# A cap of two on the expert-weight transfers in flight, in a one-core MoE encoder kernel

## The chip, the cores and the metric

The kernel runs on one core of one Trainium2 chip. The metric is the device time of one execution in microseconds (us), lower is better. Three runs of the kernel before took 1706.2, 1709.3 and 1712.2 us, so the median is 1709.3 us. The profiled execution is the one of 1706.2 us; its span from the first to the last instruction is 1704.3 us.

## The reference

One layer of an encoder over 1024 tokens of 1024 features, in float32: adaLN conditioning, a token mixer (convolution, Fourier and gating heads) and a mixture of experts. The last part is what matters here:

```python
def expert_block(args):
    xb, e = args
    return (jax.nn.silu(xb @ w1[e]) * (xb @ w3[e])) @ w2[e]
...
y = jnp.zeros((N, D), h.dtype).at[t_s].add(contrib)      # two experts per token, weighted
...
x = x + gate2 * moe(h, ...)
return rmsnorm(x, final_g)
```

There are 64 experts. Each has w1 and w3 of 1024x512 and w2 of 512x1024, so 6 MB of float32 weights per expert and 384 MB in all. Each token picks one group of eight experts and the best two in it.

## The kernel before, in words

It is written by hand with one instruction stream per engine and semaphores between them. After the mixer and the router (up to about 510 us) comes the expert phase. The tokens of an expert are cut into **blocks** of 32 rows; every expert has at least one block, and there are 106 with these inputs. The expert phase has these streams:

- **SP** loads the weights. `piece(e, slot, k)` issues one DMA of 1024 KB into one of four slots of the arena: k = 0, 1 are the halves of w1, k = 2, 3 those of w3, k = 4, 5 those of w2. The first 24 pieces (four experts) are issued while the router still works. The loop at L374 issues the other 360, six for an expert: before k = 0 it waits until TensorE has used w1 and w3 of the expert that is in the slot (`s_h13`), before k = 4 until it has used w2 (`s_yp`). Each of the 24 places has its own semaphore, `s_w[slot][k]`. Nothing else limits how many pieces are under way. Behind the loop the same stream issues the 4 MB load of x2 (L387), the final gain, and the stores of the output.
- **GpSimd** gathers the rows of a block with an indirect DMA (L443), two blocks ahead.
- **TensorE** transposes the rows, multiplies them with w1 and w3 (`up`, L677, 64 matmuls), transposes the hidden rows (L694) and multiplies the hidden rows of the block before with w2 (`down`, L688, 32 matmuls). Before `down` it waits for `s_y`, which the next stream raises.
- **VectorE** at L1215 scales the result of a block out of PSUM into `y_s`. There is one `y_s`, so it waits first for `s_yst`, the landing of the store of the block before.
- **ScalarE** applies silu, copies, and at L846 issues the store of `y_s`, 128 KB, to `ys_dram`:

```python
act.dma_start(ys_dram.ap()[bass.ds(n * BLK, BLK), :].rearrange("r (q c) -> q r c", q=4), y_s).then_inc(s_yst, 16)
```

So a block has a loop through memory: L1215, store issued, store landed, L1215 of the next block. SP's pieces travel on DMA queue q1, ScalarE's stores on q10, GpSimd's gathers on q0. After the last block a tail gathers both results of each token, adds x2, normalises and writes the output.

Of the kernel before, what the change touches and what calls it, by code (L numbers as in the profile page):

```python
# [36 lines left out]
SLOTS = 4  # L37
# [2 lines left out]
EPS = 1e-6  # L40
BANKS = 8
EARLY = 4
NEG = -3.0e38

C_ID, C_TRI, C_ONE, C_BD, C_DFT, C_EXC, C_INC, C_REV = 0, 128, 256, 384, 512, 768, 832, 896
# [20 lines left out]
def build(nc, x, c, ln1_g, ln2_g, w_ada, b_ada, w_in, w_out, conv_w, conv_b, conv_gn_g, conv_gn_b,  # L66
# [3 lines left out]
    with ctx:  # L70
        def sem(name):
            return ctx.enter_context(nc.semaphore(name))
# [16 lines left out]
        def at(offset, *shape):  # L89
            n = 1  # L90
            for s in shape:
                n *= s
            view = arena[:, offset:offset + n]
            if len(shape) == 2:
                view = view.rearrange("p (a b) -> p a b", a=shape[0])
            if len(shape) == 3:
                view = view.rearrange("p (a b c) -> p a b c", a=shape[0], b=shape[1])
            return view
# [70 lines left out]
        prob, sel, sel2, hot1, hot2, cand, ranks, before = (at(r0 + i * HALF, HALF) for i in range(8))  # L169
# [43 lines left out]
        s_w = [[sem(f"slot{i}_{what}_in") for what in ("w1a", "w1b", "w3a", "w3b", "w2a", "w2b")] for i in range(SLOTS)]  # L213
# [74 lines left out]
        def _(sp):  # L288
# [25 lines left out]
            def piece(e, slot, k):  # L314
                u, h = k // 2, k % 2
                if u < 2:
                    src = (exp_w1, exp_w3)[u][bass.ds(e, 1), h * 512:(h + 1) * 512, :].rearrange("e (q p j) f -> (e p) q (j f)", q=2, j=2)
                else:
                    src = exp_w2[bass.ds(e, 1), h * 256:(h + 1) * 256, :].rearrange("e (k p) d -> (e p) k d", k=2)
                sp.dma_start(at(slot * EXPERT_FLOATS + k * 2048, 2, D), src).then_inc(s_w[slot][k], 16)  # L320
# [53 lines left out]
            with sp.Fori(0, EXPERTS // SLOTS - 1) as r:  # L374
                for slot in range(SLOTS):

                    end = sp.value_load(table[0:1, bass.ds(r * SLOTS + (1 + slot), 1)], min_val=1, max_val=MAX_BLOCKS)
                    for k in range(6):
                        if k == 0:
                            sp.wait_ge(s_h13, end)  # L380
                        if k == 4:
                            sp.wait_ge(s_yp, end)
                        piece(r * SLOTS + (SLOTS + slot), slot, k)

            end = sp.value_load(table[0:1, EXPERTS - SLOTS + 1:EXPERTS - SLOTS + 2], min_val=1, max_val=MAX_BLOCKS)
# [343 lines left out]
        def _(act):  # L729
# [80 lines left out]
            for i in range(TILES + 1):  # L810
# [5 lines left out]
                if i >= 1:  # L816
# [6 lines left out]
                    last.then_inc(freed_a, 1)  # L823
                if i == EARLY + 1:
                    act.wait_ge(s_expin, 1)
                    part = prob[:, 0:EARLY * EXPERTS]
                    nc.scalar.activation(part, part, ACT.Exp).then_inc(s_exp, 1)
            act.wait_ge(s_expin, 2)
            part = prob[:, EARLY * EXPERTS:]
            nc.scalar.activation(part, part, ACT.Exp).then_inc(s_exp, 1)  # L830
# [50 lines left out]
        def _(dve):  # L881
            steps = [0]

            def link(ins):

                steps[0] += 1
                ins.then_inc(s_link, 1)
                dve.wait_ge(s_link, steps[0])
# [146 lines left out]
            def route(part, t0, t1):  # L1035
# [3 lines left out]
                def tiles(view):  # L1039
                    return te(view)[:, t0:t1, :]  # L1040
# [27 lines left out]
                def first_best(values, top_row, hot, where_row):  # L1068

                    link(v.tensor_reduce(groups(top_row), tge(values), AX_X, ALU.max))  # L1070
                    link(v.tensor_tensor(tge(cand), tge(values), over_pe(top_row), ALU.is_equal))
                    link(v.tensor_tensor(tiles(cand), tiles(cand), over_t(cst[:, C_REV:C_REV + EXPERTS], n), ALU.mult))
                    link(v.tensor_reduce(groups(where_row), tge(cand), AX_X, ALU.max))
                    link(v.tensor_tensor(tge(hot), tge(cand), over_pe(where_row), ALU.is_equal))

                first_best(sel, 0, hot1, 1)
                link(v.scalar_tensor_tensor(tiles(sel2), tiles(hot1), NEG, tiles(sel), ALU.mult, ALU.add))
                first_best(sel2, 2, hot2, 3)
# [16 lines left out]
            def weights(t0, t1):  # L1095

                first, second, both = (tok[:, k, t0:t1] for k in (2, 3, 4))
                picked(first, prob, hot1, t0, t1)
                picked(second, prob, hot2, t0, t1)
                link(v.tensor_tensor(both, first, second, ALU.add))  # L1100
                link(v.reciprocal(both, both))
                v.tensor_tensor(gate_w[:, 0, t0:t1], first, both, ALU.mult)
                link(v.tensor_tensor(gate_w[:, 1, t0:t1], second, both, ALU.mult))
# [9 lines left out]
            for i in range(TILES + 2):  # L1113
# [25 lines left out]
                if i == 1:  # L1139
                    dve.wait_ge(s_gate2, 128)  # L1140
                    link(v.tensor_tensor(gate2, gate2, gate2_b, ALU.add))
                if i == EARLY + 1:
                    route(0, 0, EARLY)
                    weights(0, EARLY)

# [151 lines left out]
```

## Time and profile before

| what | value |
|---|---|
| median of three runs | 1709.3 us |
| profiled execution | 1706.2 us |
| its span | 1704.3 us |
| TensorE busy | 1242.9 us, 73% |
| VectorE, ScalarE, GpSimd busy | 27%, 12%, 11% |
| q1 (SP) over the span | 471.05 MB, 71.5% of 16 DMA engines |
| q0 (GpSimd) | 32.33 MB, 5.3% |
| q10 (ScalarE) | 13.90 MB, 2.4% |
| DMA share from 517 to 1620 us | 0.95 |
| granted TensorE clock, mean | 0.856 |

The expert phase reaches from about 510 to 1660 us and the tail from there to the end. The shares of the table are means over the whole span: in the expert phase the DMA engines are near full, before it they are half idle. TensorE is busy much of the time, but a busy TensorE is not one that sets the end; that is read from the chain and from the waits.

### The profile page before, as it was taken

The numbers are of one execution on the slowest core, as the hardware profiler recorded it, in microseconds if no ns is written. First come the engines' busy times: TensorE is split into PE (matmuls) and PEld (weight loads), VectorE is DVE, ScalarE is ACT, GpSimd is POOL, SyncE is SP. The second block draws the span as 40 slices with busy tenths as digits, with TensorE's granted clock in tenths as the row PEclk, the third lists the DMA queues.
The fourth block names the chain that finished last, engine by engine and source line by source line (L and its number), as shares of the span: only waits on it lengthen the run. The fifth ranks groups of instructions, "written<-read, shape, count | busy, mean of one in ns | idle before, by whom it ended". The sixth has DMA issues, their size and how long they took to land.

```text
span 1704.3 us, 31808 instructions
## 1 busy us (share of the span) xinstructions
PE 1242.9 (73%) x12648; PEld 658.3 (39%) x12649; DVE 456.3 (27%) x880; ACT 211.8 (12%) x537; POOL 186.2 (11%) x322
## 2 busy tenths in 40 slices
PE   3899999999837676667776787776666576776670
PEld 3444555445524333333433344333333233333330
DVE  1399936133641111111111111111111111111117
ACT  1400133012201000000100011000000000000014
POOL 3011300000001111011110111110110001110113
PEclk9999999999859888787977889777888778787985
DMA  9564523432489999897999958999999999799917
GB/s 334 196 208 162 216 85 135 152 118 99 165 336 358 392 357 411 337 398 281 363 410 385 376 216 348 366 410 410 376 374 375 377 387 372 291 408 411 394 64 295
DMA packets 156232, 517.73 MB, mean 304 GB/s; under 512 B 11865, under 2 KB 28777, under 8 KB 156072
## 3 DMA queue, kind: packets, MB, share of 16 engines
q1 hardware_dynamic: 130176, 471.05, 71.5%
q0 software_dynamic: 12032, 32.33, 5.3%
q10 hardware_dynamic: 13992, 13.90, 2.4%
q8 instruction: 24, 0.39, 0.1%
q14 instruction: 8, 0.07, 0.0%
HBM read 482.22 MB, written 35.01 MB: 303 GB/s over the span
## 4 chain that ended last, share of the span: by engine, by line
DMA 62%; PE 28%; DVE 5%; SPq 2%; issue 1%; ACT 1%; ACTq 0%; POOL 0%; POOLq 0%; DVEq 0%
DMA ys_dram<-arena 57%; PE banks L543 9%; PE banks L621 6%; PE banks L571 2%; DVE arena L1215 2%; SPq L320 2%; PE banks L589 2%; PE banks L688 1%; PE banks L677 1%; DMA arena<-in_exp_w 1%; DMA arena<-xh_dram,where 1%; DMA arena<-in_w_ada 1%; PE banks L491 1%; DMA arena<-in_x 1%; PE banks L637 1%
## 5 line engine op out<-in xcount | busy, mean ns | idle before, releaser
L677 PE MATMUL banks<-arena 128*32 128x256 f32 x6784 | 435.7, 414 | 92.3 <-DMA arena<-in_exp_w 55.3
L688 PE MATMUL banks<-arena 128*32 128x256 f32 x3392 | 292.3, 503 | 249.8 <-DVE arena L1215 249.7
L677 PEld LDWEIGHTS banks<-arena 128*32 128x32 f32 x6784 | 224.6, 119 | 273.4 <-issue 155.1
L688 PEld LDWEIGHTS banks<-arena 128*32 128x32 f32 x3392 | 141.0, 137 | 347.7 <-issue 318.4
L1215 DVE TENSOR_TENSOR arena<-banks,arena 128x256 f32<-128x256 f32 x106 | 45.1, 426 | 755.5 <-DMA ys_dram<-arena 746.1
L543 PE MATMUL banks<-arena 128*128 128x512 f32 x352 | 155.5, 600 | 6.9 <-ACT arena L778 6.9
L440 POOL COPY where<-quarters 128x1 int32 (+1 forms) x108 | 19.7, 182 | 1105.8 <-ACT arena L852 936.7
L838 ACT ACTIVATE arena<-banks 128x128 f32<-128x128 f32 x106 | 29.5, 278 | 797.3 <-issue 638.4
L965 DVE SCALAR_TENSOR_TENSOR arena<-arena 128x1024 f32<-128x1024 f32 x90 | 115.6, 1285 | 3.2
L443 POOL DMA_INDIRECT arena<-xh_dram,where x108 | 104.7, 969 | 87.7 <-POOL where L440 81.7
L621 PE MATMUL banks<-arena 128*128 128x512 f32 x256 | 111.4, 593 | 1.5 <-DVE arena L998 1.5
L543 PEld LDWEIGHTS banks<-arena 128*128 128x128 f32 x352 | 66.7, 192 | 89.0 <-issue 81.7
L1209 DVE TENSOR_TENSOR arena<-arena,banks 128x128 f32<-128x128 f32 x106 | 30.8, 290 | 230.7 <-ACT arena L838 230.7
L621 PEld LDWEIGHTS banks<-arena 128*128 128x128 f32 x256 | 48.1, 190 | 60.2 <-issue 57.6
L669 PE MATMUL banks<-arena 128*128 128x128 f32 x214 | 54.3, 336 | 9.1 <-ACT arena L852 9.1
L842 ACT ACTIVATE arena<-banks 128x128 f32<-128x128 f32 x106 | 29.5, 278 | 232.4 <-PE banks L694 232.4
L669 PEld LDWEIGHTS banks<-arena 128*128 128x128 f32 x214 | 33.6, 206 | 53.2 <-issue 53.2
L852 ACT ACTIVATE arena<-arena 128x256 f32<-128x256 f32 x108 | 44.8, 414 | 62.0 <-DMA arena<-xh_dram,where 61.8
L491 PE MATMUL banks<-arena 128*32 128x128 f32 x768 | 28.5, 311 | 28.1 <-DMA arena<-in_w_ada 25.6
L1202 DVE TENSOR_TENSOR arena<-banks,arena 128x256 f32<-128x256 f32 x107 | 44.8, 419 | 9.3 <-PE banks L669 9.2
L1205 DVE TENSOR_TENSOR arena<-arena 128x256 f32<-128x256 f32 x107 | 45.7, 427 | 3.7
L694 PEld LDWEIGHTS banks<-arena 128*128 128x128 f32 x106 | 16.7, 157 | 64.7 <-issue 55.2
(201 smaller groups left out, 692.9 us busy)
## 6 DMA issues: line engine op xcount, KB each, us to landing
arena<-in_exp_w SPq DMA_DIRECT2D x384, 1024.0 KB, 20.6
arena<-in_w_ada SPq DMA_DIRECT2D x12, 2048.0 KB, 11.6
ys_dram<-arena ACTq DMA_DIRECT2D x106, 128.0 KB
ys_dram<-arena POOLq DMA_DIRECT2D x16, 512.0 KB, 10.0
arena<-in_x SPq DMA_DIRECT2D x2, 2048.0 KB, 20.7
arena<-in_dft SPq DMA_DIRECT2D x1, 4096.0 KB, 12.6
arena<-in_w_out SPq DMA_DIRECT2D x1, 4096.0 KB, 14.0
arena<-in_x SPq DMA_DIRECT2D x8, 512.0 KB, 4.2
```

The source lines that it names most:

```text
L443: pool.indirect_dma_start(out=xrow_next, out_offset=None, in_=xh_dram.ap(), in_offset=bass.IndirectOffsetOnAxis(ap=where[:, 0:1], axis=0)) ...
L491: last = pe.matmul(ps[32 * q:32 * q + 32, 0:P], c_wide[:, k, :], ada_s[:, n % 2, k, q * P:(q + 1) * P], start=(k == 0), stop=(k == CH - 1) ...
L543: last = pe.matmul(ps, w_in_s[:, k, f0:f0 + P], h_t[:, k, s * HALF:(s + 1) * HALF], start=(k == 0), stop=(k == CH - 1))
L621: last = pe.matmul(ps, y_t[:, k, i * P:(i + 1) * P], w_out_s[:, k, s * HALF:(s + 1) * HALF], start=(n == 0), stop=(n == CH - 1))
L669: last = pe.transpose(xt_p[:, j * P:(j + 1) * P], xrow[:, j:QUART:2], ident)
L677: last = pe.matmul(h_p[32 * q:32 * q + 32, 0:2 * P].rearrange("p (a b) -> p a b", a=2), xt_s[:, k % 2, k // 2, :], w13[:, :, k, q * P:(q + ...
L688: last = pe.matmul(y_p[32 * q:32 * q + 32, 0:QUART], ff_t[:, k * BLK:(k + 1) * BLK], w2[:, k, q * QUART:(q + 1) * QUART], start=(k == 0), ...
L852: nc.scalar.activation(xrow, xrow_next, ACT.Copy).then_inc(s_xcopy, 1)
L965: ins = v.scalar_tensor_tensor(y_t[:, cc, :], src, w, y_t[:, cc, :], ALU.mult, ALU.add)
L1202: v.tensor_tensor(xt_v, banks[:, 0, 0:QUART].rearrange("p (a t) -> p a t", a=CH), ab_jq[:, 0, :, :].rearrange("p j q -> p (j q)").unsqueez ...
L1205: v.tensor_tensor(xt_v, xt_v, ab_jq[:, 1, :, :].rearrange("p j q -> p (j q)").unsqueeze(2).broadcast_to([P, CH, BLK]), ALU.add).then_inc(s ...
L1215: v.tensor_tensor(y_s, banks[:, 3, 0:QUART], gate2, ALU.mult).then_inc(s_y, 1)
```

## The change

Every piece that the loop issues first waits for the landing of the piece two places before it in the order of the stream. For k of 2 to 5 that is piece k - 2 of the same expert, for k of 0 and 1 it is piece 4 or 5 of the expert before (in the slot before, and for slot 0 in slot 3 of the round before, hence the other count). So at most two pieces of the loop are under way. The loads ahead of the loop and behind it are as they were.

```diff
+AHEAD = 2
...
                         if k == 4:
                             sp.wait_ge(s_yp, end)
+
+                        before, rounds = (slot, r + 2) if k >= AHEAD else ((slot - 1) % SLOTS, r + (2 if slot else 1))
+                        sp.wait_ge(s_w[before][(k - AHEAD) % 6], rounds * 16)
                         piece(r * SLOTS + (SLOTS + slot), slot, k)
```

On SP, the body of the loop for one expert (slot 0), before. The name block_h_ready is `s_h13`, block_y_filled is `s_yp`:

```order
L320 ISA [waits block_h_ready]
L320 DMA arena<-in_exp_w1 128x2x1024
L320 ISA
L320 DMA arena<-in_exp_w1 128x2x1024
L320 DMA arena<-in_exp_w3 128x2x1024 x2
L320 DMA arena<-in_exp_w2 128x2x1024 [waits block_y_filled]
L320 DMA arena<-in_exp_w2 128x2x1024
```

Two waits for six pieces. The same place on SP after the change; slot3_w2a_in and its like are `s_w[3][4]` and its like:

```order
L386 ISA [waits block_h_ready]
L321 ISA [waits slot3_w2a_in]
L321 DMA arena<-in_exp_w1 128x2x1024
L321 ISA [waits slot3_w2b_in]
L321 DMA arena<-in_exp_w1 128x2x1024
L386 ISA
L321 DMA arena<-in_exp_w3 128x2x1024 [waits slot0_w1a_in]
L321 DMA arena<-in_exp_w3 128x2x1024 [waits slot0_w1b_in]
L321 DMA arena<-in_exp_w2 128x2x1024 [waits slot0_w3a_in,block_y_filled]
L321 DMA arena<-in_exp_w2 128x2x1024 [waits slot0_w3b_in]
```

No DMA has moved and none was added; each of the six has a wait for a landing ahead of it. The lists of the other engines differ in line numbers alone.

## Rows read from the trace of the kernel before

**Rows 1.** The page's chain that ended last, shares of the span.
```profile
DMA ys_dram<-arena 57%; PE banks L543 9%; PE banks L621 6%; PE banks L571 2%; DVE arena L1215 2%; SPq L320 2%; PE banks L589 2%; PE banks L688 1%; PE banks L677 1%; DMA arena<-in_exp_w 1%; DMA arena<-xh_dram,where 1%; DMA arena<-in_w_ada 1%; PE banks L491 1%; DMA arena<-in_x 1%; PE banks L637 1%
```

**Rows 2.** Waits, 515 to 1640 us: total us, times, longest us.
```profile
DVE arena L1215 <- DMA ys_dram<-arena: 742.6, 96, 9.6
...
PE banks L677 <- DMA arena<-in_exp_w: 55.3, 9, 10.3
```

**Rows 3.** The chain in order of time: start us, length us, what.
```profile
562.99 11.09 DMA ys_dram<-arena
574.71 10.57 DMA ys_dram<-arena
...
804.74 8.80 DMA ys_dram<-arena
...
1653.59 3.32 DMA ys_dram<-arena
```

**Rows 4.** Issue to landing of the 384 weight pieces, us.
```profile
DMA to landing us min/median/max: 4.9/20.6/24.5
```

**Rows 5.** DMA queues, 802 to 803 us: packets, MB, share of 16 engines.
```profile
q10 hardware_dynamic: 86, 0.09, 25.2%
```

**Rows 6.** DMA queues, 563 to 566.8 us.
```profile
q1 hardware_dynamic: 403, 1.55, 102.1%
```

**Rows 7.** DMA queues, 566.8 to 573.5 us.
```profile
q1 hardware_dynamic: 647, 2.49, 92.2%
q10 hardware_dynamic: 130, 0.13, 5.5%
```

**Rows 8.** DMA queues, 804 to 805 us, then 804.7 to 808.8 us.
```profile
DMA packets 0, 0.00 MB, mean 0 GB/s; under 512 B 0, under 2 KB 0, under 8 KB 0
...
q1 hardware_dynamic: 305, 1.19, 90.3%
```

**Rows 9.** Issue to landing of the pieces issued at 452.5 and at 804.0 us.
```profile
DMA to landing us min/median/max: 4.9/4.9/4.9
...
DMA to landing us min/median/max: 5.3/5.3/5.3
```

**Rows 10.** The same for the piece issued at 455.2, and two at 456.1 and 456.7.
```profile
DMA to landing us min/median/max: 13.1/13.1/13.1
...
DMA to landing us min/median/max: 17.3/18.2/19.2
```

**Rows 11.** The same for the pieces issued at 1490.6 and 1595.9 (37 later).
```profile
DMA to landing us min/median/max: 16.6/16.6/16.6
...
DMA to landing us min/median/max: 21.5/21.5/21.5
```

**Rows 12.** The same for the pieces issued at 518.2 and 1599.1 (358 later).
```profile
DMA to landing us min/median/max: 8.8/8.8/8.8
...
DMA to landing us min/median/max: 20.8/20.8/20.8
```

**Rows 13.** Stores issued, 1500 to 1615 us, then 517 to 1614 us.
```profile
ys_dram<-arena ACTq DMA_DIRECT2D x10, 128.0 KB
...
ys_dram<-arena ACTq DMA_DIRECT2D x99, 128.0 KB
```

**Rows 14.** Issue to landing of the piece issued at 1593.6 us (k = 3 of the last expert).
```profile
DMA to landing us min/median/max: 20.4/20.4/20.4
```

**Rows 15.** TensorE in order of time, the last expert: start us, length us.
```profile
1621.90 3.66 PE L677 MATMUL banks<-arena 128*32 128x256 f32 x64
...
1633.85 4.37 PE L677 MATMUL banks<-arena 128*32 128x256 f32 x64
...
1640.71 3.66 PE L677 MATMUL banks<-arena 128*32 128x256 f32 x64
...
1646.86 3.66 PE L677 MATMUL banks<-arena 128*32 128x256 f32 x64
```

**Rows 16.** Issue of the x2 load, us to landing (issued at 1602.7 us).
```profile
arena<-x_dram SPq DMA_DIRECT2D x1, 4096.0 KB, 28.9
```

## The prediction

> **What bounds the kernel now.** I read the chain of waits first. Stores of block results hold 57% of it, and the weight pieces 1% [rows 1]. The waits say the same: in the expert phase VectorE's L1215 waits 742.6 us, 96 times, for the landing of the store before it, while TensorE waits only 55.3 us, 9 times, for weights [rows 2]. So the expert phase is a loop of store after store. A store that meets a full stream of weights takes 10.6 to 11.1 us from its issue to its landing, and the next starts 11.7 us after the one before; the store at 1653.59, with no weights under way, takes 3.3 us [rows 3]. The reader is to see that 128 KB cost 11 us because of what else is on the DMA engines.
>
> The second view is the queues. A weight piece lands 20.6 us after its issue in the median [rows 4], though pieces land 2.55 us apart (the piece of 455.2 lands at 468.3, that of 456.7, three later, at 475.9 [rows 10]). So some eight are under way, and the cap of two binds nearly always.
>
> What a store shares with them: alone on the queues it keeps 25.2% of 16 engines busy [rows 5], that is four engines, 86 packets in 1 us, 0.046 us each. Its 128 packets are thus 32 on each of four engines, 1.5 us of their time. A weight piece is 256 packets, 16 on each of 16 engines, 2.55 us, so 0.16 us each. In the first 3.8 us after the store of 562.99 no packet of q10 is served, and q1 has 403 [rows 6]; then q10 serves 130 within 6.7 us against 647 of q1 [rows 7]. On the four engines that is close to one for one: 32 pairs of 0.16 + 0.046 make 6.6 us. So a store first stands behind what those engines have already taken in (a store alone reaches them about 1.2 us after its issue, which leaves some 2.7 us, 17 packets of q1), then alternates with q1 for 31 more. By this, a store costs 3.3 + 48 x 0.16 = 11.0 us; the rows say 10.6 to 11.1.
>
> The four engines are also the bound of the weight stream. From the landing at 1507.2 to that at 1617.4 there are 37 pieces in 110.2 us [rows 11] and ten stores [rows 13]: 110.2 - 37 x 2.55 = 15.9, so 1.6 us for a store with its gather. The whole stream, 358 pieces from 526.9 to 1619.9 [rows 12], takes 1093 us; 358 x 2.55 = 913, and 99 stores [rows 13] x 1.6 = 158; the remaining 22 us are idle. For one expert (six pieces, 1.65 stores) the engines need 15.3 + 2.6 = 17.9 us, and the store loop 1.65 x 11.7 = 19.3 us. The two bounds lie close, the store loop slightly on top.
>
> **The change part by part.** Nothing but 360 waits on SP is new. Queued behind such a wait are the later pieces, and at the end the x2 load; no other engine's work stands on SP.
>
> *The store.* With two pieces under way, the four engines never hold more than 32 packets of q1. The landing is told about 0.5 us after the last data (4.9 us for a piece alone [rows 9], of which 1.0 us passes before the first packet, since there is none from 804 to 805 [rows 8], about 0.9 for the first, and 15 x 0.16). So at a landing 13 packets of the next piece are left; the new piece arrives 1.1 us later, when 6 are left. The backlog swings between 6 and 22, about 13 in the mean, where it was always above 17. While it is under 17 the store's packets fill the free places ahead of the next piece, about 10 of them; the other 22 alternate. So the store waits for 13 + 22 = 35 packets of q1 and not 48: 3.3 + 35 x 0.16 = 8.9 us, and the loop 9.5 us. Bounds: it could stay at 11.1, or come down to near 3.3. The nearest row is the store of 804.74, issued with just two pieces under way: 8.80 us [rows 3]. But those two were not followed by a third, and its first packet also came late, after 305 packets of q1 [rows 8], 19 on an engine.
>
> With a loop of 9.5 us, an expert needs 1.65 x 9.5 = 15.7 us of stores, under the 17.9 of the DMA engines. So the weights become the bound. The gain is not 96 x 2.2 us = 211 us but what the stream leaves idle: 22 us, of which I keep 5 for the stretches with many blocks for one expert. **-17 us.**
>
> *The handover.* A piece is issued when the one two ahead has landed, so two pieces take one latency and the wake of SP. A piece alone takes 4.9 to 5.3 us [rows 9]; SP I take at 0.1. That is 2.50 to 2.70 us for a piece against 2.55, a cost of 0 to 0.15, mean 0.08. While a store is on the four engines a piece takes 3.3 us and the new one comes in time, so nothing is lost. Stores cover some 60% of the time (6 of 10 us), which leaves 143 pieces: 143 x 0.08 = **+11 us**, bounds 0 and 21 (358 x 0.15 = 54 if the stores hide none of it).
>
> *The end.* The last expert's piece k = 3 lands at 1614.0 [rows 14], but its four up products start at 1621.9, 1633.9, 1640.7 and 1646.9 [rows 15]: the first 7.9 us late, behind the store loop, the second 12 us after it, the others at the 6.2 us that TensorE needs. With the faster loop the first starts as its piece lands; the second still meets the 4 MB x2 load, which lands at 1631.6 [rows 16], so I give it 10.5; then 7 and 6.2. The last starts 24 us after the landing and not 33: **-9 us**.
>
> Sum: -17 + 11 - 9 = -15. The profiled execution took 1706.2 us (span 1704.3), so 1691.2. It is 3 us under the median of the runs shown, 1709.3; I let the forecast stand between and say 1692.
>
> Here the rule that speaks against the change: the Trainium skill ("DMA: Bandwidth & Descriptors", Latency and other measured facts) says that the HBM access latency is 0.2 us in the mean and 2 us at high load, and that it makes up most of a DMA's fixed cost. No row here shows a piece that was issued alone into a loaded memory. By that rule the handover would be dearer than I take it, which is the first rival. The fit of the same page of the Trainium skill (Anatomy of one DMA, made for transfers that GpSimd issues), 2.0 us plus the bytes at 436 GB/s, would make it 4.4 us for a piece, an estimate, and the handover free.
>
> **The rivals.**
>
> *The queue runs dry (slower).* If the latency of a piece issued at a landing is longer under load than the 5.3 us of rows 9, each pair waits for it, in the stretches with stores too. With 6.3 us for a pair, 3.15 us for a piece, it is +0.6 x 143 = 86 us, less the 26 gained: 1766. The point from which it decides is 26 us: 0.18 us per piece outside stores, or 0.07 over all 358. For it: the margin is thin, 6 packets or 1 us of work when the new piece arrives, and the first packet of a piece takes 0.9 us. Against it: the range 4.9 to 5.3 includes exactly that. I take 1720 to 1770, centre 1735.
>
> *The store stays as it is.* If what a store waits for is only what the engines have taken in, and two pieces fill that (19 packets an engine were ahead of it with two under way [rows 8]), the loop stays near 11 us. Then the gains fall away and the handover stays: 1706 + 0 to 11, about 1711. Against it: the alternation needs a backlog behind the 17, and with two pieces there often is none.
>
> *The gain is larger.* If the handover is free and the stretches of idle go altogether: 1706.2 - 22 - 13 = 1671. Below that it can't go, since the engines' 913 + 158 us remain. Against it: three favourable ends at once.
>
> *The cap doesn't bind.* Excluded by the median of 20.6 us [rows 4]; no chance given.
>
> **How the numbers follow.** Forecast (1680 to 1702) 0.52; larger gain (1665 to 1680) 0.10; store unchanged (1703 to 1718) 0.17; queue runs dry (1715 to 1770) 0.21. What a measurement can tell from no change is 0.3%, 5 us: under 1704 is faster, over 1714 slower. Faster takes the first two and a sliver of the third: 0.63. Same: 0.14 from the third. Slower: 0.23. The range must leave out no more than 0.2: 1674 to 1728 leaves out part of the larger gain (0.04) and the upper part of the dry queue (0.14). The forecast's own range is 1680 to 1702.
>
> **What would show it.** Right: the pieces' median landing falls from 20.6 to 5 to 6 us; the stores in the chain take 8 to 9.5 us; L1215's wait for stores falls from 743 to below 500 us, and TensorE's wait for weights rises from 55 to over 150 us; pieces land 2.6 us apart outside stores, and the stream from 526.9 ends at about 1614. Wrong: stores still at 11 us (second rival), or stores shorter but pieces 2.8 us or more apart where no store is on, and the last landing later than 1620 (first rival). The DMA share of the expert phase would then fall, since the other twelve engines stand with the four.

## The result and the profile after

The changed kernel is slower. It takes 1834.5 us (1820.6 to 1842.3, 4 runs) against 1709.7 us (1706.2 to 1712.2, 4 runs), a ratio of 1.0727 [1.0673, 1.0781] (the brackets behind a ratio are its 95% interval). Thirteen more executions of the changed kernel took 1820.3 to 1854.8, so a capped kernel varies by some 1% from run to run, and the one before by 0.2%. I had said 1692, with a range up to 1728. Of the cases, the first rival had the direction ("the queue runs dry", 1720 to 1770), but its upper end too was short by 64 us.

The page of the changed kernel: the chain that ended last, which was 57% stores and 1% weights before [rows 1].

```profile
DMA arena<-in_exp_w 65%; PE banks L547 8%; PE banks L625 6%; PE banks L575 2%; PE banks L593 2%; DMA arena<-xh_dram,where 1%; PE banks L681 1%; PE banks L495 1%; DMA arena<-in_w_ada 1%; DMA ys_dram<-arena 1%; DMA arena<-in_x 1%; PE banks L641 1%; PE banks L692 1%; DVE arena L1249 0%; DVE arena L1244 0%
```

The weights have taken the chain from the stores. The waits of the changed kernel, 515 to 1790 us (total us, times, longest us), say the same. L681 and L1219 are the lines 677 and 1215 of before, moved by the four new lines:

```profile
PE banks L681 <- DMA arena<-in_exp_w: 430.1, 41, 15.5
DVE arena L1219 <- DMA ys_dram<-arena: 310.9, 63, 9.2
...
ACT arena L856 <- DMA arena<-xh_dram,where: 85.8, 41, 5.2
```

TensorE's wait for weights grew from 55.3 to 430.1 us, and VectorE's wait for stores fell from 742.6 to 310.9 [rows 2]. So the stores did get shorter, or at least less waited for, and it was no use. The weight pieces issued in the loop, and their time from issue to landing (20.6 us in the median before [rows 4]):

```profile
L321 SPq DMA_DIRECT2D arena<-in_exp_w x360: 15/373/386, 516.3 to 1755.5; - x180
...
DMA to landing us min/median/max: 4.8/7.0/9.3
```

The last issue is 359 pieces and 1239.2 us after the first: 3.45 us for a piece, where before it was 1093 / 358 = 3.05 [rows 12]. That is the whole loss. The last issue (k = 5 of the last expert) is released by the landing of the last expert's piece k = 3. It landed at 1614.0 before [rows 14], and now at 1755.5: +141.5 us. From there to the end of the span it was 1704.3 - 1614.0 = 90.3 us and is 1837.1 - 1755.5 = 81.6: -8.7. The sum, +132.8, is the difference of the two spans.

Where a piece loses its time is seen in the chain in order of time (start us, length us, what) of the changed kernel. Each row is a step from a landing to the landing of the piece that it released, so it moves two pieces:

```profile
612.17 7.36 DMA arena<-in_exp_w
...
619.55 5.36 DMA arena<-in_exp_w
...
625.07 5.20 DMA arena<-in_exp_w
...
630.28 8.73 DMA arena<-in_exp_w
...
639.03 5.04 DMA arena<-in_exp_w
...
644.23 4.92 DMA arena<-in_exp_w
...
649.17 7.17 DMA arena<-in_exp_w
...
656.36 7.52 DMA arena<-in_exp_w
```

Two kinds of step stand there. Four take 4.9 to 5.4 us, which is what 2 x 2.55 us of work need. The others take 7.2 to 8.7. The step of 8.73 us has a store in it (issued at 629.59) and a gather (630.83). I sorted all 358 such steps, from each issue to the next but one, by whether packets of a store or of a gather were served in them (worked out from the trace's packets): 218 have both, 7.3 us in the mean; 53 a store alone, 6.4; the other 87, nearly all with neither, 6.2. My sum had 6.6 for a step with a store and 5.26 without.

The DMA queues (packets, MB, share of 16 engines) of the changed kernel: at 623 to 626 us, ahead of that step and with no store on; inside it at 630.5 to 634.5, the store's first part; and at 635.1 to 635.9, just behind the issue of 634.94.

```profile
q1 hardware_dynamic: 313, 1.22, 102.9%
...
q1 hardware_dynamic: 363, 1.42, 94.5%
q10 hardware_dynamic: 100, 0.10, 7.4%
...
q1 hardware_dynamic: 18, 0.07, 22.4%
q10 hardware_dynamic: 8, 0.01, 2.9%
q0 software_dynamic: 4, 0.00, 1.5%
```

The reader is to see the last three rows: q1 falls to 22.4% of 16 engines, near the share of four. The trace has no engine numbers, so that they are the store's four is read from the share. The piece issued at 627.45 is told landed only just ahead of 634.94, 7.5 us later, since the issue of 634.94 waited for it. By then the packets show (worked out from the trace) that all but about four engines have run out of the next piece too, at about 634.5; the first packets of the newly issued one come at 636.0. So for 1.5 us twelve engines have nothing to do but a gather's packets, because the landing was held back by the four. Those first packets then take up to 0.89 us each, where a packet of q1 takes 0.16 in the median. Over the whole phase it shows in one row of the windows (after the length: busy us of PE, PEld, DVE, ACT and POOL, granted clock, DMA share, GB/s), first of the changed kernel and then of before:

```profile
517.00:1752.00 1235.00, 736.66 (x9999) 381.63 (x9999) 149.17 (x405) 92.50 (x304) 117.62 (x204) 0.78 0.92 325
```

```profile
517.00:1620.00 1103.00, 766.62 (x9997) 396.65 (x9993) 149.43 (x405) 89.33 (x304) 116.58 (x203) 0.83 0.95 369
```

The same matmuls and blocks, at 325 GB/s for 369. The share says more than that (worked out from the packets): of the 132 us that the window is longer, the engines stand for 52 and are busy for 80 with the same bytes. The 80 are long packets: about 4460 of q1 take over 0.3 us, 0.60 in the mean, where the kernel before has 1209. What they take over 0.16 us comes to 122 us for each engine, and to 33 before. The clock's fall from 0.83 to 0.78 is not the cause: TensorE is busy for 0.60 of the time and waits for data.

### The profile page after: what moved, and what is told of

Its sections match the earlier page's. It is cut to its first block, busy times and chain, and to the rows that moved or that the text cites. A ratio compares the mean times of both kernels' runs of the same rounds, so it can differ in the third digit from the quotient of the medians.

```text
span 1837.1 us, 31943 instructions
## 1 busy us (share of the span) xinstructions
PE 1213.9 (66%) x12648; PEld 643.2 (35%) x12649; DVE 456.3 (25%) x880; ACT 215.1 (12%) x537; POOL 186.7 (10%) x322
## 4 chain that ended last, share of the span: by engine, by line
DMA 69%; PE 25%; DVE 3%; issue 1%; ACT 1%; SPq 0%; POOL 0%; POOLq 0%; ACTq 0%; DVEq 0%
DMA arena<-in_exp_w 65%; PE banks L547 8%; PE banks L625 6%; PE banks L575 2%; PE banks L593 2%; DMA arena<-xh_dram,where 1%; PE banks L681 1%; PE banks L495 1%; DMA arena<-in_w_ada 1%; DMA ys_dram<-arena 1%; DMA arena<-in_x 1%; PE banks L641 1%; PE banks L692 1%; DVE arena L1249 0%; DVE arena L1244 0%
## 5 line engine op out<-in xcount | busy, mean ns | idle before, releaser
L681 PE MATMUL banks<-arena 128*32 128x256 f32 x6784 | 484.8, 448 | 462.3 <-DMA arena<-in_exp_w 430.1
L681 PEld LDWEIGHTS banks<-arena 128*32 128x32 f32 x6784 | 242.9, 128 | 671.8 <-issue 574.6
L692 PE MATMUL banks<-arena 128*32 128x256 f32 x3392 | 220.4, 403 | 37.2 <-DVE arena L1219 37.0
L692 PEld LDWEIGHTS banks<-arena 128*32 128x32 f32 x3392 | 108.9, 114 | 108.4 <-issue 50.2
L1219 DVE TENSOR_TENSOR arena<-banks,arena 128x256 f32<-128x256 f32 x106 | 45.1, 426 | 360.0 <-DMA ys_dram<-arena 310.9
L547 PEld LDWEIGHTS banks<-arena 128*128 128x128 f32 x352 | 66.7, 192 | 86.3 <-issue 81.9
L625 PEld LDWEIGHTS banks<-arena 128*128 128x128 f32 x256 | 48.1, 190 | 60.2 <-issue 57.9
L673 PEld LDWEIGHTS banks<-arena 128*128 128x128 f32 x214 | 33.6, 206 | 60.2 <-issue 49.6
L575 PE MATMUL banks<-arena 128*128 128x384 f32 x128 | 41.4, 486 | 0.0
## 6 DMA issues: line engine op xcount, KB each, us to landing
ys_dram<-arena POOLq DMA_DIRECT2D x16, 512.0 KB, 10.2
```

Source lines behind the costliest of these rows:

```text
L547: last = pe.matmul(ps, w_in_s[:, k, f0:f0 + P], h_t[:, k, s * HALF:(s + 1) * HALF], start=(k == 0), stop=(k == CH - 1))
L575: last = pe.matmul(ps[:, 0:SGU], h_t[:, k, i * P:(i + 1) * P], w_in_s[:, k, 1024 + SGU:WIN], start=(k == 0), stop=(k == CH - 1))
L625: last = pe.matmul(ps, y_t[:, k, i * P:(i + 1) * P], w_out_s[:, k, s * HALF:(s + 1) * HALF], start=(n == 0), stop=(n == CH - 1))
L673: last = pe.transpose(xt_p[:, j * P:(j + 1) * P], xrow[:, j:QUART:2], ident)
L681: last = pe.matmul(h_p[32 * q:32 * q + 32, 0:2 * P].rearrange("p (a b) -> p a b", a=2), xt_s[:, k % 2, k // 2, :], w13[:, :, k, q * P:(q + ...
L692: last = pe.matmul(y_p[32 * q:32 * q + 32, 0:QUART], ff_t[:, k * BLK:(k + 1) * BLK], w2[:, k, q * QUART:(q + 1) * QUART], start=(k == 0), ...
```

## The experiments

Two theories stood against each other. **A, unequal engines:** the store and the gather load some of the 16 DMA engines more than others; with two pieces under way those that are behind hold back the landing, the others run dry, and the 1 us of work that they have left is too little to cover it. **B, a fixed price:** the wait at each landing, or a latency that grows under load, costs some 0.4 us a piece, whatever else is on the engines.

**How many pieces.** AHEAD is the only edit; all waits stay.

```
-AHEAD = 2
+AHEAD = 3        (and, in the second kernel, 4)
```

> The cap of the change at 3 pieces instead of 2, nothing else. With the cap of 2 pairs of pieces take 7.3 us where a store and a gather run beside them (5.8 where none does), and the time is 1834 us. Theory A (unequal engines: a store lies on 4 of 16 engines and puts them behind, the landing waits for the last engine while the others run dry): a third piece gives every engine 2.55 us more of work, more than the 2 us by which engines drift, so most of the loss goes: pieces 3.0 us apart, about 1700 us. Theory B (a fixed latency of 7.1 us from issue to landing, divided by the number under way): 7.1/3 = 2.4 us, less than the 2.55 that the data take, so all of the loss goes and the shorter store stays: about 1690 us. If both are wrong and the loss is in SP's waits themselves, about 1830.

> The cap at 4. Theory A and theory B both: no loss of the stream is left; stores meet a backlog of more than 17 packets again and take 10.5 to 11 us, so 1700 to 1710 us, not told from the kernel before. If the waits themselves cost, over 1750.

Measured: 1710.9 us with three (ratio to before 0.9998 [0.9983, 1.0013]) and 1710.9 with four (0.9993 [0.9978, 1.0008]). The waits and landings with three, 515 to 1765 us:

```profile
DVE arena L1219 <- DMA ys_dram<-arena: 771.0, 98, 9.9
...
PE banks L681 <- DMA arena<-in_exp_w: 33.0, 6, 10.5
```

```profile
DMA to landing us min/median/max: 4.8/8.8/10.8
```

One piece more takes away the whole loss, and with it the form of B in which a wait costs something by itself: the same 360 waits cost nothing here. Both theories had the loss gone, so this run does not choose between them otherwise. It also takes away the gain, for which I had 1700 and 1690 on record. With 8.8 us to a landing the stores are waited for as long as before. None of the caps tried has both, a full stream and shorter stores.

**The store's shape.** The store's outer dimension has 4 elements. Here it has 128; the rows are then written in another order, which the result doesn't undo.

```
-act.dma_start(ys_dram.ap()[...].rearrange("r (q c) -> q r c", q=4), y_s)
+act.dma_start(ys_dram.ap()[...].rearrange("r (q c) -> (r q) c", q=4), y_s)
```

> The changed kernel (cap 2) with each block's result stored as one run of 128 rows of 1 KB, whose outer dimension is 128 instead of 4, so that it goes over 16 engines; the rows of the result land permuted, the bytes and their number are the same. Theory A: a store now takes 8 packets, 0.4 us, of every engine alike, so no engine is put behind: pairs with a store and a gather fall from 7.3 to about 6 us, the stream of 360 pieces from 1239 to about 1080 us, the time to about 1680 us. Theory B: the latency of a piece isn't due to where the store lies; pairs stay near 7 us and the time near 1800 us.

> The kernel before (no cap) with the same wide store. Both theories: the store takes 17 packets of q1 ahead plus 8 pairs, 1.2 + 2.7 + 8 x 0.2 + 0.7 = 6.2 us instead of 11, the loop 6.8 us; the stream needs 913 us + 99 x 0.7 (8 packets of the store and 2 of the gather per engine) = 982 us instead of 1093 with the idle of the long clusters. So about 1706 - 80 = 1625 us. If the four engines are not what bounds the stream, the time stays above 1680 us.

Measured: with the cap 1627.5 us (0.9521 [0.9458, 0.9583]), without it 1584.7 (0.9257 [0.9235, 0.9279]). The same bytes on 16 engines and not on four take 207 us from the capped kernel and 125 from the one before, where A had 1680 and 1625: the direction is A's, but both gains are 40 to 53 us larger than I had worked out. Waits, landings and chain of the capped one, the chain over the same part of the work:

```profile
PE banks L681 <- DMA arena<-in_exp_w: 298.3, 42, 11.3
...
DVE arena L1219 <- DMA ys_dram<-arena: 51.1, 28, 4.0
```

```profile
DMA to landing us min/median/max: 4.9/5.5/8.4
```

```profile
658.34 4.90 DMA arena<-in_exp_w
...
663.40 4.98 DMA arena<-in_exp_w
...
668.39 5.42 DMA arena<-in_exp_w
...
673.83 5.74 DMA arena<-in_exp_w
...
679.73 5.66 DMA arena<-in_exp_w
```

The steps of 7 to 9 us are rare now and the median landing falls from 7.0 to 5.5 us, with the same cap, the same waits and more bytes a second. So most of the loss is not a fixed price. It depends on where the store lies. But a cost of the cap stays that the store's shape doesn't explain, 1627.5 - 1584.7 = 43 us.

**Without the store, without the gather, without both.** The rows of the result are zeroed ahead of the phase, and a semaphore is raised in place of the store. For the gather, the blocks compute on stale rows.

```
-act.dma_start(ys_dram.ap()[...].rearrange("r (q c) -> q r c", q=4), y_s).then_inc(s_yst, 16)
+act.sem_inc(s_yst, 16)
-pool.indirect_dma_start(out=xrow_next, ..., in_=xh_dram.ap(), ...).then_inc(s_xrow, 16)
+pool.sem_inc(s_xrow, 16)
```

> The changed kernel (cap 2) without the stores of the block results in the expert phase (the semaphore is raised at once; the result rows are zeroed before the phase instead, 16 more 512 KB stores beside the mixer), so the result lacks the experts. Theory A (unequal engines): without the narrow store the pairs fall as they did with the wide one, from 7.3 to 5.9 us with a gather and to 5.0 without, and the time to about 1620 us. If the store only adds its own 1.5 us of work on four engines, which its wide form shares out, then 1836 us - 99 x 1.5 = 1685 us.

> The changed kernel (cap 2, narrow store) without the gathers of the blocks' rows (the semaphore is raised at once; every block computes on stale rows, the counts of blocks are the same). A gather is 2 packets, 0.32 us, of each engine. If it costs only that, 99 x 0.32 = 32 us less: 1805 us. If it costs what the pairs say (those with a store and a gather take 7.3 us, with a store alone 6.6, so 0.7 us for each pair that it touches, two pairs for most gathers), 0.7 us x 99: 1765 us. Theory A expects the latter or less, since the gather's packets too reach the engines at different times.

> The changed kernel (cap 2) with neither stores nor gathers in the expert phase. Only the weights are on the queues. Theory A: the handover itself is free, pairs take 5.05 us, as between stores with the wide store, and the stream of 360 pieces 905 us; the last block about 25 us later: 1706 - 190 = about 1510 us. The theory that each handover of two leaves a gap of its own (0.4 us per piece) gives 1050 us for the stream, 1650 us in all.

Measured, all with the cap of two: 1600.6 us without the store (0.9360 [0.9328, 0.9391]), 1767.2 and 1793.7 without the gather (two runs), 1561.1 and 1591.6 without both. So the store costs 1834 - 1601 = 234 us and the gather, beside it, 41 to 67; two runs so far apart don't tell its size better. For the kernel without the store I had 1620 by A and 1685 for a store that costs only its own 1.5 us. The waits without the gather:

```profile
PE banks L680 <- DMA arena<-in_exp_w: 376.4, 41, 16.0
...
DVE arena L1218 <- DMA ys_dram<-arena: 272.1, 61, 8.9
```

I had 1510 us on record for the kernel without both; it took 51 to 82 us more. The queues of it (the run of 1591.6), 515 to 1515 us, in 40 slices and in sum:

```profile
GB/s 299 378 406 406 406 395 399 346 304 343 308 342 386 364 385 405 404 407 408 404 398 390 322 371 407 409 349 325 349 318 383 405 357 371 369 408 403 393 399 409
DMA packets 97448, 375.78 MB, mean 376 GB/s; under 512 B 5728, under 2 KB 5728, under 8 KB 97442
```

Nothing but weights is on the engines here, and still the stream holds its 405 to 409 GB/s only in some stretches and has 300 to 350 in others. A step of two pieces takes 5.25 us in the median but 5.57 in the mean (2.78 for a piece), and 41 of 358 take 6.5 us or more (18 take 7). So two pieces are not enough even without any other load. That the engines can be kept full through the phase shows in a kernel further below, with three pieces under way and with stores and gathers spread over 16 engines. In 39 of 40 slices from 520 to 1490 us it stays at 401 GB/s or more (`cap3_four_stores`):

```profile
GB/s 401 410 409 409 409 410 409 409 409 408 409 409 410 409 409 409 409 409 380 410 409 409 409 408 409 408 409 409 409 408 409 409 409 408 409 409 409 409 410 409
```

A has no cause for the dips with two, unless the engines get out of step by themselves; B has one, if a latency comes and goes that a third piece hides. These runs don't tell the two apart.

**How much on the four engines.** The store still goes over four engines, but only the first 256 bytes of each 1024-byte row are written (the rest stays zero).

```
-...rearrange("r (q c) -> q r c", q=4), y_s)
+...rearrange("r (q c) -> q r c", q=4)[:, :, 0:QUART // 4], y_s[:, 0:QUART // 4])
```

> The changed kernel (cap 2) with the narrow store over the same four engines, but only the first quarter of each 1 KB row stored: 32 packets of 256 bytes an engine (the result rows are zeroed before the phase, so the result lacks the rest). Theory A: the four engines fall behind by some 0.5 us a store instead of 1.5, less than the margin of 1 us, so most of the loss goes: 1610 to 1650 us, near the wide store's 1628. If the number of packets or the fact of a store over four engines is what costs, and not how long it holds them, it stays above 1750 us.

Measured: 1643.3 us (0.9602 [0.9546, 0.9658]), two runs.

```profile
PE banks L681 <- DMA arena<-in_exp_w: 324.6, 42, 14.8
...
DVE arena L1219 <- DMA ys_dram<-arena: 68.6, 32, 6.9
```

By load on the four engines: none 1601, a quarter of the bytes 1643, all 1834 (1.5 us a store). The first quarter costs 43 us, the rest 191. A packet of 256 bytes takes 18 ns on its engine and one of 1024 takes 46 (medians of q10, worked out from the trace), so the small store holds its four engines for 32 x 0.018 = 0.6 us and the whole one for 1.5. The price is thus not in proportion: 0.6 us cost 43, and 0.9 us more cost 191. That is the steep rise that A expects where the hold grows past the 1 us of work that the other engines have left; one point in between doesn't show where it begins. It is not the number of packets, which is the same.

**Pieces of twice the size.** Two pieces of 2 MB under way hold the work of four of 1 MB.

```
-for k in range(6): ... piece(..., slot, k)
+for u in range(3): ... double(..., slot, u)      # 2 MB, one semaphore
```

> The changed kernel with the loop's pieces doubled to 2 MB (a whole w1, w3 or w2 of an expert in one DMA) and the cap still at two pieces. The store is the narrow one. Theory A (what matters is the work that each engine still has when a landing is told, against the drift between engines): 5.1 us of work remain, as with a cap of three of the small pieces, so no loss: about 1711 us. The rival, that two transfers under way are too few whatever their size because of the wait and the issue of each: half as many handovers at the same price each, 1709 + 125 / 2 = 1772 us.

Measured: 1748.4 us (1.0228 [1.0198, 1.0258]), slower than before by 2.3% and faster than the change. A had 1711 and the rival 1772. Its waits:

```profile
DVE arena L1226 <- DMA ys_dram<-arena: 811.3, 100, 10.4
PE banks L688 <- DMA arena<-in_exp_w: 27.2, 4, 10.8
```

TensorE waits 27.2 us for weights, so the stream is not what bounds it any more, as A says. But the store loop is longer than with three pieces of 1 MB: 811 us of waits and not 771, which is the 38 us between the two kernels. From its issue to its last packet a store takes 9.9 us in the mean here and 9.5 there (worked out from the packets), and there are about 100 of them. What makes it longer beside 2 MB pieces I did not find out.

**The complete kernel with a spread store.** Four DMAs of 32 rows of 1 KB put the same data at the same place over 16 engines, and their semaphore goes up by 64.

```
-act.dma_start(ys_dram.ap()[bass.ds(n * BLK, BLK), :].rearrange("r (q c) -> q r c", q=4), y_s).then_inc(s_yst, 16)
+for q in range(4):
+    act.dma_start(ys_dram.ap()[bass.ds(n * BLK, BLK), q * QUART:(q + 1) * QUART], y_s[32 * q:32 * q + 32, :]).then_inc(s_yst, 16)
```

> The kernel before (no cap), its result stored correctly by four DMAs of 32 rows each, one for each quarter of the columns, each over 16 engines (2 packets an engine), all landed before the buffer is written again. Theory A: the same 8 packets on every engine as the wide store, which took 1585 us, but ScalarE now issues four DMAs of 0.55 us, 1.65 us more in the loop of a block: stream near 982 us as before it, loop about 8.5 us, so 1590 to 1610 us. If four small DMAs cost more on the engines than one (each has its own semaphore packets and restarts), up to 1650 us.

> The cap at 3 and each result stored by four DMAs of 32 rows over all 16 engines (the version that took 1585 us without a cap); a complete kernel. Theory A: with no engine put behind and 5.1 us of work left at a landing the stream loses nothing; it took 991 us uncapped. Waits for gathers (167 us) and stores (184 us) may shrink with the backlog, but PE's wait for weights is the bound, so 1575 to 1590 us. If a cap has a cost of its own at any depth: 1600 to 1625 us.

> The cap at 2 and each result stored by four DMAs of 32 rows over all 16 engines: a complete kernel, the fourth corner beside the kernel before (1709), the change (1834) and four stores without a cap (1585). Theory A: the price of the cap falls from 125 us to what gathers and chance leave, as with the wide store, 43 us: about 1628 us, within 15. If each of the four store DMAs disturbs the 16 engines at another time, more: up to 1660 us. If the cap costs the same wherever the store lies: 1710 us.

Measured: 1585.0 us without a cap (0.9271 [0.9249, 0.9293]), 1585.6 with a cap of three (0.9268 [0.9242, 0.9293]), 1653.7 with two (0.9640 [0.9600, 0.9681]). All compute the whole reference, and the first, for which I had 1590 to 1610, beats both kernels of this case, the one before by 7.3%. Its waits and a window of it (columns as above; the kernel before has 0.95 and 366 GB/s in the same window, the changed one 0.91 and 323):

```profile
PE banks L677 <- DMA arena<-in_exp_w: 245.5, 37, 10.8
...
DVE arena L1216 <- DMA ys_dram<-arena: 183.6, 70, 4.4
ACT arena L853 <- DMA arena<-xh_dram,where: 167.3, 69, 4.1
```

```profile
520.00:1490.00 970.00, 689.29 (x9899) 361.63 (x9899) 147.23 (x399) 93.23 (x298) 115.31 (x199) 0.85 1.03 408
```

The wait for stores falls from 742.6 us [rows 2] to 183.6, and the stream runs at 408 GB/s, which is 1 MiB in 2.57 us: nothing is left for a cap to give. ScalarE pays for the four issues, one row of its timeline:

```profile
700.21 1.75 ACTq L847 DMA_DIRECT2D ys_dram<-arena  x4
```

The one issue took 0.56 us. The 1.2 us more are less than what each store saves. With two pieces, waits again:

```profile
PE banks L681 <- DMA arena<-in_exp_w: 324.3, 41, 15.1
...
DVE arena L1220 <- DMA ys_dram<-arena: 96.8, 54, 4.0
```

The price of a cap of two is thus 125 us with the narrow store, 69 with four spread ones and 43 with one; that of a cap of three is nothing with either. I had 1628 for the kernel behind the second of these, and up to 1660 in case four DMAs disturb the engines more than one with the same bytes. They do, by 26 us at a cap of two and by nothing without a cap (1585.0 and 1584.7), and I can't say why.

## Why the prediction was wrong

**What bounds the kernel: right.** Stores bound the loop, the four engines the stream close behind it. The experiment with a spread store shows both at once: the loop and the stream shrink together, and 125 us go. With the cap of three, where the stream is whole again, stores bound the loop as before. I had counted the 158 us that the stores and gathers take from the stream and left them alone, as a given.

**The store gets shorter: right in direction, and more than I had.** I had 11.0 us down to 8.9, by 2.1. From its issue to its last packet on the queue a store took 10.2 us before and takes 7.4 now (medians, worked out from the trace's packets), 2.8 less. The wait ahead of L1219 fell from 7.7 us in the mean to 310.9 / 63 = 4.9. For the loop I had 9.5 us; where it still waits it varies, as these rows of VectorE in the changed kernel show, 8.4 and 11.7 us apart (start, length, in brackets the wait):

```profile
1017.78 0.43 DVE L1219 TENSOR_TENSOR arena<-banks,arena 128x256 f32<-128x256 f32 x1 [5.36 <-DMA ys_dram<-arena]
1026.21 0.43 DVE L1219 TENSOR_TENSOR arena<-banks,arena 128x256 f32<-128x256 f32 x1 [5.52 <-DMA ys_dram<-arena]
1037.88 0.43 DVE L1219 TENSOR_TENSOR arena<-banks,arena 128x256 f32<-128x256 f32 x1 [8.77 <-DMA ys_dram<-arena]
```

**What the stream leaves idle, -17: it did not come.** It needed a stream that is full. The stream was no longer full, so the term went with the next one.

**The handover, +11: mis-sized, and the step that failed.** It reads: "While a store is on the four engines a piece takes 3.3 us and the new one comes in time, so nothing is lost." With it went "143 x 0.08" for the pieces outside the stores. Together with the -17 they gave a stream of 3.03 us a piece, 6.06 a step: 60% of the steps at 6.6 and 40% at 5.26. The steps measured are 76% with a store, at 7.14 in the mean, and 24% without, at 6.2 (6.91 over all). Per step that is

- 0.76 x (7.14 - 6.6) = 0.41 us because a step with a store is longer than the four engines' work,
- 0.24 x (6.2 - 5.26) = 0.23 because steps without one are longer too,
- 0.16 x (6.6 - 5.26) = 0.21 because more steps have a store in them than I had counted,

0.85 us in sum, and over 179.5 steps 73 + 41 + 38 = 152 us on top of my stream, which had the +11 and the -17 in it. My forecast of the profiled span was 1704.3 - 15 = 1689.3 us, and it is 1837.1, 148 more: these three terms account for it within a few us.

The first is the quoted step. The new piece comes in time for the four engines, which have a store's work on top of the piece's. It does not for the other twelve: the landing waits for the four, which need up to 1.5 us more, and 1.5 us is more than the 1 us of work left. So the twelve stand, which the rows at 635.1 show. The experiments show the cause from two sides: the loss goes with a third piece, and most of it goes when the store is spread or left out.

That twelve engines stand would alone leave the step at the pace of the four, 6.6 us; that these lose time as well is shown by the 7.14. What they lose it to is in part seen: the 80 us of longer packets are more than the 52 us of standing. A piece that finds empty engines has long first packets (0.70 to 1.1 us for the one issued at 804.0 in the kernel before, up to 0.89 for the one at 634.94 above), and the more often engines run dry, the more of these there are. I had this 0.9 us in the time of a lone piece, and nothing for engines that run dry inside the stream. That all the long packets are such restarts fits, but isn't shown.

For the second term, the kernel with neither store nor gather has 5.57: a lone piece's 4.9 to 5.3 us [rows 9], on which 0.08 rested, is too short for a step inside a stream, by 0.3 us of the 0.9.

**The end, -9: right in sum, by luck in its parts.** The four blocks of the last expert now start their up products 0.4 us after the landing at 1755.4 and then as here, TensorE in the changed kernel:

```profile
1755.82 5.26 PE L681 MATMUL banks<-arena 128*32 128x256 f32 x64 [9.90 <-DMA arena<-in_exp_w]
...
1763.58 3.66 PE L681 MATMUL banks<-arena 128*32 128x256 f32 x64
...
1769.73 3.66 PE L681 MATMUL banks<-arena 128*32 128x256 f32 x64
...
1779.38 3.74 PE L681 MATMUL banks<-arena 128*32 128x256 f32 x64
```

The last starts 23.9 us after the landing; I had 24. The steps in between are 7.8, 6.2 and 9.7 us, where I had 10.5, 7 and 6.2, so the errors cancel: the long store (11.0 us, issued at 1764.15) holds back the fourth block and not the second.

**The first rival** had the right outcome and a quarter of the mechanism, a latency that grows under load and costs most where no store is on. Its mark, 2.8 us or more a piece where no store is on, did come (3.1), but that is a quarter of the loss; most of it lies where the store is. The mark that named the cause is the last one: the DMA share falls, because twelve engines stand with the four. I wrote that sentence without asking what it does to the sum.

Two of my signs of being right came as well (VectorE's wait for stores below 500 us, at 310.9, and TensorE's for weights over 150, at 430.1): they were no use, since the slower outcome has them too.

Of the rule of the Trainium skill ("DMA: Bandwidth & Descriptors", Latency and other measured facts), 2 us of memory latency at high load, the weights alone show no constant sign: their median step of 5.25 us, in stretches at 406 GB/s, is no longer than with a lone piece's latency. The stretches at 300 to 350 GB/s it might explain; no run here tells.

**The second rival** (store unchanged, about 1711) is what a cap of three and of four do. In the rival with the larger gain the sum has 13 us for the end, where the part on the end has 9, and gives no row for it; nothing hangs on it.

## What to carry to other kernels

Ask of a cap on transfers under way whether it leaves each DMA engine, at a landing, more work than the engines differ by; the emptiest engine counts and not the mean backlog. Here two pieces of 1 MB were too few, even with nothing else on the engines, and three enough. These are two points of one kernel and no threshold. Before shaping a queue, look at how many engines each DMA lies on: a row of the queues at a moment when one is alone shows it (25.2% was four of 16), and spreading that store was worth 125 us, more than any cap.

## What the runs showed of the hardware

A store whose outer dimension has 4 elements lies on four engines, one of 128 on all. While it is alone on the queues, the one of 128 has this row (the kernel without a cap, 1540.0 to 1540.3 us):

```profile
q10 hardware_dynamic: 98, 0.09, 87.4%
```

From issue to landing a store alone takes 3.3 us on four engines [rows 3] and 1.7 on 16 (the last one of that kernel, issued at 1539.0). The Trainium skill ("DMA: Bandwidth & Descriptors", Why a DMA increments its semaphore by 16 and not by 1) says that a DMA goes over as many engines, up to 16, as divide the outermost sizes of both sides; the trace agrees, with 25.2% for the one of four [rows 5] and 87.4% for the one of 128. For the DMAs of 32 rows it has only the stream of 408 GB/s. I had not expected its price on a full stream: 128 KB in 1.5 us of four engines cost 125 us over 100 stores, 1.25 us each, close to the full time of the four, in the kernel before. A store beside a stream without a cap was waited for 7.7 us in the mean on four engines, and 183.6 / 70 = 2.6 us on 16.
